# Seven-product down projection: product order, row scaling inside the last products, and weight sums on GpSimd

## The chip, the cores and the metric

The kernel runs on one core of one Trainium2 chip. The metric is the device time of one execution in microseconds. Three runs of the kernel before gave 2259.54, 2260.1 and 2260.4, median 2260.1.

## The reference, cut to what matters

One layer of a hybrid streaming encoder: a mixer (gated linear attention and retention), a residual, and a ConvFFN with a residual. The change touches only the end of the ConvFFN, for 1024 rows (SEQ) of 1024 columns (D_MODEL) and D_FF = 2816:

```
f = gelu(u_gate) * u_val
x = x + rmsnorm(f @ w_ffn_down, ln_post_ffn)
```

with `rmsnorm(y, w) = y * rsqrt(mean(y*y) + eps) * w` over the 1024 columns of a row.

## The kernel before, in words

**Seven products.** The down projection f @ w_ffn_down is done by the Strassen-Winograd scheme with seven products of half-size blocks in place of eight. f is cut into four blocks (rows 0 to 511 and 512 to 1023, D_FF halves), the weights into b11, b12, b21, b22 (D_FF halves by column halves of 512), the result into c11, c12 (rows 0 to 511) and c21, c22. A product is a sum over KH = 11 slices of 128 of D_FF. One slice of one product is a step; 77 steps (DOWN_STEPS) run in the order of DOWN_ORDER, s = 0 to 76, and `down_product(s)` gives product and slice.

**A step.** Every fp32 operand is split in a high and a low part (fp32r), and a step on TensorE is 4 groups of 128 rows (tok), each with three matmuls of 128x512 (`product3`, L433 to L435): high by high, high by low, low by high. So a step is twelve matmuls. Its parts lie in slot s % 4 of the ring w_hi and w_lo (RING = 4): ScalarE writes the high parts of weights (`w_high`, L2999) and of f (`x_high`, L3012) once the step four before is done on TensorE; VectorE writes the low parts (`w_low` L3031, `x_low` L3017; for the first steps GpSimd does the weights' in `w_low_pool` L3023).

**Sums.** Products 5, 6, 7 and 3 need sums of f blocks (`x_sum`, L3050, VectorE), products 5, 6, 7 and 4 sums of weight blocks (`w_sum`, L3069), one 128x512 subtraction a slice, written in place. VectorE does the weight sums in the order of `w_sums_at`: product 5's from step 8 on, two a step; 7's from step 13; 6's from step 21; 4's from step 56. The counters s_sum, u_sum, slab_ready, d_lo and d_hi tell the engines what is done.

**Banks.** A product accumulates in four PSUM banks, one a tok, X_BANKS or Z_BANKS. They are read out one at a time some steps behind the product: products 1 and 5 copied by ScalarE (`copies`, L3081), the others added by VectorE (`evict`, L3135 to L3146) into d_out, a view of the tile act_f. Product 4's banks are read at the very end (L3188).

**Loads.** SyncE's queue runs through `down_sp`: for each step the load of f (`x_load`, which waits until x_low of the step four before is done), and at fixed steps the rows of b22 (13 to 23, into act_f) and b21 (33 to 43, into d_b21). At step 50 it issues the residual rows, 2 MB into d_x0, waits until they are landed, and issues 2 MB more into d_x1. The eight output stores follow the last x load. f itself is stored to the scratch ffn_scratch by `f_store`, the last two blocks of it (20 and 21) from ScalarE's queue.

**Before step 8.** The up projection's last blocks run on VectorE (`taps`, `f`) between the first x_low. `up_act`, `up_dve`, `up_pool` and `up_sp` write this order out by hand; GpSimd ends there, with w_low of steps 0 to 7. Steps from 8 on are in `down_act`, `down_dve` and `down_sp`.

**The order DOWN_ORDER = (1, 5, 6, 3, 7, 2, 4).** Rows 512 to 1023 right half (c22) are done with product 7 (steps 44 to 54), rows 0 to 511 with product 2 (55 to 65), and the left half of rows 512 to 1023 (c21) with product 4 (66 to 76). For each group of 128 rows ScalarE squares the row and takes mean and root (L3087, L3094, L3098), VectorE multiplies with the weights of the norm (`weighted`, L3155), takes the reciprocal (L3150), and scales and adds the residual (`residual`, L3158). ScalarE squares the c22 halves (`half_mean`) at steps 62 to 65, and VectorE multiplies them there. The whole rows 0 to 511 (`first_rows`) are handled behind step 76, the left halves of the lower rows behind them, each as eviction on VectorE, square on ScalarE, product, reciprocal and residual on VectorE.

**The end of product 4.** TensorE runs its last four steps (73 to 76) tok by tok, so that tok 0 is done first.

Of the kernel before, what the change touches and what calls it, by code (L numbers as in the profile page):

```python
# [30 lines left out]
P = 128  # L31
# [80 lines left out]
RING = 4  # L112
# [91 lines left out]
def build(nc, x, positions, w_stream, w_dec, b_dec, ln_post_mix, ln_post_ffn, ln_cols_in, conv_in,  # L204
          ident_in, interval_in, masks_in, ret_dec_in, ret_q_in, ret_k_in, inv_freq_in, eps_in, out):
    ctx = ExitStack()
    with ctx:
# [2626 lines left out]
        def w_operand(s):  # L2834

            i, k = down_product(s)
            return {1: b11, 5: b11, 6: b11, 7: b12, 3: lambda k: d_b22[:, k, :],
                    2: lambda k: d_b21[:, k, :], 4: lambda k: d_b21[:, k, :]}[i](k)
# [18 lines left out]
        W_SUMS = [what for s in range(DOWN_STEPS) for what in w_sums_at(s)]  # L2857

        def t_sums_done(i, k):

            return AFTER_ROWS["u_sum"] + sum_count(FT - 1, 4) + W_SUMS.index((i, k)) + 1

        def evicted(i, tok, second=0):

            return {6: 2 * tok + second, 3: 8 + tok, 7: 12 + 2 * tok + second, 2: 20 + tok, 4: 24 + tok}[i] + 1
# [82 lines left out]
        def down_bank(i, tok):  # L2948
            return psum[:, (X_BANKS if i in (1, 6, 7, 4) else Z_BANKS)[tok], :]

        def down_pe(pe):
# [11 lines left out]
            def bank_free(i, tok):  # L2963
# [88 lines left out]
        def w_sum(dve, i, k):  # L3052

            if i == 5:
                dve.wait_ge(sem["slab_ready"], SL_DOWN + down_at(1, k) + 1)
                o, a, b = b11(k), b12(k), b11(k)
            elif i == 6:
                dve.wait_ge(sem["slab_ready"], SL_DOWN + down_at(5, k) + 1)
                w_landed(dve, "b22", k)
                o, a, b = b11(k), d_b22[:, k, :], b11(k)  # L3060
            elif i == 7:
                w_landed(dve, "b22", k)
                dve.wait_ge(sem["u_sum"], t_sums_done(5, k))
                o, a, b = b12(k), d_b22[:, k, :], b12(k)
            else:
                dve.wait_ge(sem["slab_ready"], SL_DOWN + down_at(2, k) + 1)
                dve.wait_ge(sem["u_sum"], t_sums_done(6, k))
                o, a, b = d_b21[:, k, :], d_b21[:, k, :], b11(k)
            nc.vector.tensor_tensor(o, a, b, ALU.subtract).then_inc(sem["u_sum"], 1)  # L3069

        def down_act(act):

            def copies(s):

                tok = (s - RING) % KH
                i = DOWN_ORDER[(s - RING) // KH - 1]
                if s < KH + RING or tok >= 4 or i not in (1, 5):
                    return
                rows = slice(HALF, D) if i == 5 else slice(0, HALF)
                step_done(act, s - RING - tok - 1)  # L3080
                nc.scalar.activation(d_out[:, (4 if i == 5 else 0) + tok, rows], down_bank(i, tok), ACT.Copy  # L3081
                                     ).then_inc(sem["u_s1"], 1)
# [8 lines left out]
            def half_mean(tok):  # L3091
                act.wait_ge(sem["d_evac"], evicted(7, tok))
                square(tok, d_out[:, 4 + tok, HALF:], 48 + tok)
# [7 lines left out]
            def first_rows(t):  # L3101
                act.wait_ge(sem["d_evac"], evicted(2, t))
                square(4 + t, d_out[:, t, :], 24 + t)
                deviation(t, eps_col[:, 0:1])

            for s in range(POOL_STEPS, DOWN_STEPS):
# [13 lines left out]
        def down_dve(dve):  # L3120
            every, first, second = slice(0, D), slice(0, HALF), slice(HALF, D)

            def evict(s):

                tok = (s - RING) % KH
                i = DOWN_ORDER[(s - RING) // KH - 1]
                if s < KH + RING or tok >= 4 or i not in (6, 3, 7, 2):
                    return
                step_done(dve, s - RING - tok - 1)
                o = down_bank(i, tok)  # L3130
                c11, c12 = d_out[:, tok, first], d_out[:, tok, second]
                c21, c22 = d_out[:, 4 + tok, first], d_out[:, 4 + tok, second]
                if i == 6:
                    dve.wait_ge(sem["u_s1"], AFTER_ROWS["u_s1"] + FT + 4 + tok + 1)
                    nc.vector.tensor_tensor(c21, o, c11, ALU.add).then_inc(sem["d_evac"], 1)  # L3135
                    dve.wait_ge(sem["d_evac"], evicted(6, tok))
                    nc.vector.tensor_tensor(c22, c22, c21, ALU.add).then_inc(sem["d_evac"], 1)
                elif i == 3:
                    dve.wait_ge(sem["d_evac"], evicted(6, tok, 1))
                    nc.vector.tensor_tensor(c12, o, c22, ALU.add).then_inc(sem["d_evac"], 1)  # L3140
                elif i == 7:
                    dve.wait_ge(sem["d_evac"], evicted(3, tok))
# [18 lines left out]
            for s in range(POOL_STEPS, DOWN_STEPS):  # L3161
# [4 lines left out]
                w_low(dve, s)  # L3166
                x_low(dve, s)
                for i, k in w_sums_at(s):
                    w_sum(dve, i, k)
                evict(s)  # L3170
                tok = s - down_at(2) - 7
                if 0 <= tok < 4:
                    dve.wait_ge(sem["d_sq"], NT + tok + 1)
                    weighted(tok, d_out[:, 4 + tok, second], d_out[:, 4 + tok, second], second)
            for t in range(4):
                dve.wait_ge(sem["d_sq"], NT + 4 + t + 1)
                weighted(4 + t, d_out[:, t, :], d_out[:, t, :], every)
            dve.wait_ge(sem["d_x_in"], 16 * MG + 32)
            for t in range(4):
                rstd(t)  # L3180
                dve.wait_ge(sem["d_scaled"], NT + 4 + t + 1)
                residual(t, d_x0, every)
# [114 lines left out]
        def up_sp(sp):  # L3297
# [18 lines left out]
            for s in range(RING, POOL_STEPS):  # L3316
# [15 lines left out]
        def up_pool(pool):  # L3332
# [111 lines left out]
        def up_act(act):  # L3444
# [58 lines left out]
            f_store(act, FT - 2)  # L3503
# [7 lines left out]
            f_store(act, FT - 1)  # L3511
# [11 lines left out]
        def up_dve(dve):  # L3523
# [96 lines left out]
            x_low(dve, RING + 3)  # L3620
            f(FT - 1)
# [141 lines left out]
```

## Time and profile before

| | us |
|---|---|
| median of three runs | 2260.1 |
| the profiled execution | 2260.02 |
| its span | 2257.8 |
| last stretch without a matmul | 20.2 |

| engine, over the whole span | busy us | share |
|---|---|---|
| TensorE, matmul (PE) | 2193.3 | 97% |
| TensorE, weight load (PEld) | 1813.0 | 80% |
| VectorE (DVE) | 1301.1 | 58% |
| ScalarE (ACT) | 713.8 | 32% |
| GpSimd (POOL) | 1433.5 | 63% |

How to read it: the span is cut by engine and by line of the kernel. The down projection takes the last 244 us, from 2014 on. Matmuls are pipelined: one is 0.39 us long in the records, and the next begins 0.23 later, so the starts are to be read, not the lengths. The same holds in part for VectorE, ScalarE and GpSimd, whose instructions overlap the next by some hundredths. `x2` is two instructions merged in one row, with the time of both. What stands in brackets is idle time of the engine before the row, and what ended it.

### The profile page before, as it was taken

How to read it: one execution, taken by the hardware profiler on the slowest of the kernel's cores; microseconds unless marked ns; L12 is line 12 of the kernel's file. 1: busy time of each engine (PE TensorE's matmuls, PEld its weight loads, DVE VectorE, ACT ScalarE, POOL GpSimd, SP SyncE). 2: the span in 40 equal slices, each digit the busy share in tenths (PEclk: the TensorE clock that was granted, in tenths of full speed). 3: DMA queues.
4: the chain of work that ended last, by engine and by line, in shares of the span. 5: the costliest groups of instructions: out<-in, count | busy, mean ns of one | idle time of the engine just before them, and what ended most of it. 6: DMA issues, size and time to landing. Idle time of an engine off the chain costs nothing. (4 is left out here: it accounts for less than half of the span.)

```text
span 2257.8 us, 27976 instructions
## 1 busy us (share of the span) xinstructions
PE 2193.3 (97%) x10354; PEld 1813.0 (80%) x10354; DVE 1301.1 (58%) x1612; ACT 713.8 (32%) x1155; POOL 1433.5 (63%) x946
## 2 busy tenths in 40 slices
PE   8999999999999999999998999999899999999996
PEld 7888888889778888877775888878778888877875
DVE  7322222222626666678887443333967777779976
ACT  4323333321222222212223111015444444444443
POOL 5787777766456555489764478860999999960000
PEclk9999999999999999999999999999999999999998
DMA  4233333323372333366556566643122222346642
GB/s 180 97 118 104 112 112 109 107 94 112 115 247 89 126 122 126 99 198 183 178 176 199 189 209 230 217 163 121 66 75 84 84 84 85 93 177 210 200 168 109
DMA packets 182613, 314.14 MB, mean 139 GB/s; under 512 B 13072, under 2 KB 93200, under 8 KB 182480
## 3 DMA queue, kind: packets, MB, share of 16 engines
q1 hardware_dynamic: 182048, 311.25, 42.4%
q8 instruction: 84, 1.38, 0.3%
q10 hardware_dynamic: 432, 1.11, 0.1%
q14 instruction: 49, 0.40, 0.1%
HBM read 222.14 MB, written 90.18 MB: 138 GB/s over the span
## 5 line engine op out<-in xcount | busy, mean ns | idle before, releaser
L433 PE MATMUL psum<-act_hi,w_hi 128*128 128x512 f32 x1272 | 505.3, 397 | 4.8 <-DVE act_lo L2291 1.4
L435 PE MATMUL psum<-act_hi,w_lo 128*128 128x512 f32 x1272 | 497.0, 391 | 0.0
L434 PE MATMUL psum<-act_lo,w_hi 128*128 128x512 f32 x1272 | 496.1, 390 | 0.0
L433 PEld LDWEIGHTS psum<-act_hi,w_hi 128*128 128x128 f32 x1272 | 239.4, 188 | 56.0 <-issue 2.9
L435 PEld LDWEIGHTS psum<-act_hi,w_lo 128*128 128x128 f32 x1272 | 239.2, 188 | 51.0
L434 PEld LDWEIGHTS psum<-act_lo,w_hi 128*128 128x128 f32 x1272 | 239.6, 188 | 46.7
L467 POOL TENSOR_TENSOR w_hi<-w_raw,zero_col 128x1024 fp32r<-128x1024 f32 x53 | 108.9, 2055 | 173.6 <-PE psum L435 154.9
L470 POOL TENSOR_TENSOR w_lo<-w_raw,w_hi 128x1024 fp32r<-128x1024 f32 x53 | 144.3, 2723 | 4.2
L1074 POOL TENSOR_TENSOR w_lo<-w_raw,w_hi 128x512 fp32r<-128x512 f32 x80 | 105.0, 1313 | 65.0 <-ACT w_hi L1032 65.0
L433 PE MATMUL psum<-w_hi,act_hi 128*128 128x512 f32 (+1 forms) x384 | 139.7, 364 | 1.7 <-POOL w_lo L470 1.4
L434 PE MATMUL psum<-w_lo,act_hi 128*128 128x512 f32 (+1 forms) x384 | 139.3, 363 | 0.0
L435 PE MATMUL psum<-w_hi,act_lo 128*128 128x512 f32 (+1 forms) x384 | 139.2, 363 | 0.0
L1584 POOL TENSOR_TENSOR k_lev<-e_t,g_x 128x896 f32<-128x896 f32 x32 | 67.3, 2103 | 104.6 <-DVE q_g L1663 64.1
L433 PE MATMUL psum<-w_hi 128*128 128x512 f32 x308 | 122.3, 397 | 8.2 <-DVE w_lo L3017 7.7
L3366 POOL TENSOR_TENSOR w_lo<-w_raw,w_hi 128x512 fp32r<-128x512 f32 x80 | 126.5, 1592 | 2.9 <-ACT w_hi L3431 2.8
L433 PE MATMUL psum<-a_sums,w_hi 128*128 128x512 f32 x320 | 124.5, 389 | 0.0
L434 PE MATMUL psum<-a_sums,w_hi 128*128 128x512 f32 x320 | 124.5, 389 | 0.0
L435 PE MATMUL psum<-a_sums,w_lo 128*128 128x512 f32 x320 | 124.5, 389 | 0.0
L434 PE MATMUL psum<-w_lo,w_hi 128*128 128x512 f32 x308 | 121.3, 394 | 0.0
L435 PE MATMUL psum<-w_hi,w_lo 128*128 128x512 f32 x308 | 121.1, 393 | 0.0
L2291 DVE TENSOR_TENSOR act_lo<-a_raw,act_hi 128x512 fp32r<-128x512 f32 x48 | 55.0, 1172 | 94.7 <-ACT act_hi L2285 94.3
L433 PE MATMUL psum<-s_hi,w_hi 128*128 128x512 f32 x264 | 103.5, 392 | 4.6 <-POOL w_lo L3366 2.1
(356 smaller groups left out, 5094.1 us busy)
## 6 DMA issues: line engine op xcount, KB each, us to landing
w_raw<-in_w_stream SPq DMA_DIRECT2D x181, 512.0 KB, 4.4
proj_scratch<-stage SPq DMA_DIRECT2D x40, 512.0 KB, 5.2
r_x<-proj_scratch SPq DMA_DIRECT2D x64, 256.0 KB, 3.7
w_raw<-ffn_scratch SPq DMA_DIRECT2D x55, 256.0 KB, 2.7
value_scratch<-stage SPq DMA_DIRECT2D x24, 512.0 KB, 3.6
proj_scratch<-side_out SPq DMA_DIRECT2D x48, 256.0 KB, 2.4
w_raw<-ffn_scratch SPq DMA_DIRECT2D x22, 512.0 KB, 4.2
ffn_scratch<-u_lin_v SPq DMA_DIRECT2D x20, 512.0 KB, 5.8
```

The lines of the kernel that those rows point to most:

```text
L433: nc.tensor.matmul(o, s_hi, m_hi, start=start, stop=False)
L434: nc.tensor.matmul(o, s_hi, m_lo, start=False, stop=False)
L435: return nc.tensor.matmul(o, s_lo, m_hi, start=False, stop=stop)
L467: nc.gpsimd.tensor_tensor(w_hi[:, j, :], w_raw[:, j, :], zero_col[:, :].to_broadcast((P, D)), ALU.add).then_inc(sem["hi_split"], 1)
L470: nc.gpsimd.tensor_tensor(w_lo[:, j, :], w_raw[:, j, :], w_hi[:, j, :].bitcast(F32), ALU.subtract).then_inc(sem["slab_ready"], 1)
L1074: nc.gpsimd.tensor_tensor(w_lo8[:, n % 8, :], row_block(p, i), w_hi8[:, n % 8, :].bitcast(F32), ALU.subtract).then_inc(sem["u_lo"], 1)
L1584: nc.gpsimd.tensor_tensor(by_chunk(k_lev, b), level_decays(b), every_level(key), ALU.mult).then_inc(sem["g_klev"], 1)
L2291: nc.vector.tensor_tensor(lo, a_raw[:, i % RING, :], hi.bitcast(F32), ALU.subtract).then_inc(sem["a_lo"], 1)
L3366: nc.gpsimd.tensor_tensor(w_lo8[:, n % 8, :], block_raw(p, i), w_hi8[:, n % 8, :].bitcast(F32), ALU.subtract).then_inc(sem["u_lo"], 1)
```

## The change

1. DOWN_ORDER becomes (1, 5, 6, 3, 2, 7, 4): product 2 now at steps 44 to 54, product 7 at 55 to 65. Products 1, 6, 2, 4 use the X banks, 5, 3, 7 the Z banks, and the banks of each lie in neighbouring pairs.
2. GpSimd splits the low parts of the weights up to step 10 (POOL_STEPS = 11), and then makes all weight sums, in `w_sum`, two slices an instruction (128x1024; the eleventh slice alone, 128x512): 24 instructions in place of 44 on VectorE. The sum for product 4 goes into b11's place and no longer into b21's.
3. ScalarE's copies and VectorE's evictions read two banks at once, 1024 wide.
4. The rows of the residual are loaded 128 at a time, four loads at steps 48 to 51 and four at 56 to 59, none waiting for another.
5. Squares and roots of rows 0 to 511 (`first_rows`) are at steps 61 to 64, their multiplications at 62 to 65, reciprocal and residual at 66 to 69. The squares of the c22 halves and their multiplications are behind step 76.
6. The stores of f blocks 20 and 21 go from ScalarE's queue to SyncE's, behind the x loads of steps 9 and 11. x_low of step 8 is put ahead of f of block 21 on VectorE.

```diff
-        DOWN_ORDER = (1, 5, 6, 3, 7, 2, 4)
+        DOWN_ORDER = (1, 5, 6, 3, 2, 7, 4)
-        X_BANKS, Z_BANKS = (6, 7, 1, 2), (3, 0, 4, 5)
-        POOL_STEPS = 2 * RING
+        X_BANKS, Z_BANKS = (6, 7, 0, 1), (2, 3, 4, 5)
+        EARLY_STEPS = 2 * RING
+        POOL_STEPS = 11
+        IN_X = (1, 6, 2, 4)
...
+        def b1_pair(k):
+
+            if k < 2:
+                return d_b1_first[:, 0:2, :]
+            return d_b1_mid[:, k - 2:k, :] if k < 10 else d_b1_last[:, :].unsqueeze(1)
...
-        def w_sums_at(s):
-
-            at = [(5, k) for k in range(KH) if k // 2 == s - POOL_STEPS]
-            at += [(i, s - start) for i, start in ((7, KH + 2), (6, 2 * KH - 1), (4, 5 * KH + 1))
-                   if start <= s < start + KH]
-            return at
...
+        W_SUMS_AT = {9: ((5, 0), (5, 2)), 10: ((5, 4), (5, 6)), 11: ((5, 8),), 12: ((5, 10),),
+                     16: ((7, 0),), 18: ((7, 2),), 20: ((7, 4),), 45: ((7, 6),), 47: ((7, 8),), 49: ((7, 10),),
+                     21: ((6, 0),), 23: ((6, 2),), 25: ((6, 4),), 27: ((6, 6),), 29: ((6, 8),), 31: ((6, 10),),
+                     46: ((4, 0),), 48: ((4, 2),), 50: ((4, 4),), 52: ((4, 6),), 53: ((4, 8),), 54: ((4, 10),)}
+        W_SUMS = [what for s in sorted(W_SUMS_AT) for what in W_SUMS_AT[s]]
...
-        def residual_rows(sp, hf):
-            sp.dma_start((d_x1 if hf else d_x0)[:, :, :],
-                         x1_d[hf * HALF:hf * HALF + HALF, :].rearrange("(t p) d -> p t d", p=P)
+        def residual_rows(sp, t):
+            sp.dma_start((d_x1 if t >= 4 else d_x0)[:, t % 4, :], x1_d[t * P:(t + 1) * P, :]
...
+                if s in (9, 11):
+                    f_store(sp, FT - 2 if s == 9 else FT - 1)
...
-                if s == 4 * KH + RING + 2:
+                if 4 * KH + 4 <= s < 4 * KH + 8:
+                    sp.wait_ge(sem["s_sum"], s_sums(3, KH - 1))
+                    residual_rows(sp, s - 4 * KH)
+                if 5 * KH + 1 <= s < 5 * KH + 5:
                     sp.wait_ge(sem["slab_ready"], SL_DOWN + 4 * KH)
                     sp.wait_ge(sem["u_sum"], t_sums_done(7, KH - 1))
-                    sp.wait_ge(sem["s_sum"], s_sums(3, KH - 1))
-                    residual_rows(sp, 0)
-                    sp.wait_ge(sem["d_x_in"], 16 * MG + 16)
-                    residual_rows(sp, 1)
+                    residual_rows(sp, s - 5 * KH - 1)
...
+        def w_sum(pool, i, k):
+
+            n = min(2, KH - k)
+            slab = b1_pair(k)
+            first, second = slab[:, :, 0:HALF], slab[:, :, HALF:]
+            b22, b21 = d_b22[:, k:k + n, :], d_b21[:, k:k + n, :]
             if i == 5:
+                pool.wait_ge(sem["slab_ready"], SL_DOWN + down_at(1, k + n - 1) + 1)
+                o, a, b = first, second, first
             elif i == 6:
+                pool.wait_ge(sem["slab_ready"], SL_DOWN + down_at(5, k + n - 1) + 1)
+                for m in range(k, k + n):
+                    w_landed(pool, "b22", m)
+                o, a, b = first, b22, first
             elif i == 7:
+                for m in range(k, k + n):
+                    w_landed(pool, "b22", m)
+                pool.wait_ge(sem["u_sum"], t_sums_done(5, k))
+                o, a, b = second, b22, second
             else:
+                for m in range(k, k + n):
+                    w_landed(pool, "b21", m)
+                pool.wait_ge(sem["slab_ready"], SL_DOWN + down_at(6, k + n - 1) + 1)
+                pool.wait_ge(sem["u_sum"], t_sums_done(6, k))
+                o, a, b = first, b21, first
-            nc.vector.tensor_tensor(o, a, b, ALU.subtract).then_inc(sem["u_sum"], 1)
+            nc.gpsimd.tensor_tensor(o, a, b, ALU.subtract).then_inc(sem["u_sum"], 1)
...
-                if down_at(2) + 7 <= s < down_at(2) + 11:
-                    half_mean(s - down_at(2) - 7)
-            for t in range(4):
-                first_rows(t)
+                if 61 <= s < 65:
+                    first_rows(s - 61)
+            for tok in range(4):
+                half_mean(tok)
...
             for s in range(POOL_STEPS):
                 w_low_pool(pool, s)
+            for i, k in W_SUMS:
+                w_sum(pool, i, k)
...
             gelu(FT - 2)
             w_high(act, RING + 1)
             x_high(act, RING + 1)
-            f_store(act, FT - 2)
...
             x_low(dve, RING + 3)
+            x_low(dve, EARLY_STEPS)
             f(FT - 1)
```

## Rows read from the trace of the kernel before

**Rows 1.** Busy time by stretch: from:to, length, each engine's busy us, PEclk, DMA share, GB/s

```profile
2041.23:2080.56 39.33, 39.19 (x168) 31.28 (x169) 39.13 (x66) 17.64 (x33) 0.00 (x0) 1.00 0.77 255
2161.26:2166.31 5.05, 5.05 (x12) 3.96 (x13) 5.05 (x9) 1.78 (x3) 0.00 (x0) 0.52 0.50 156
2166.31:2237.64 71.33, 71.16 (x313) 58.30 (x311) 53.88 (x84) 36.80 (x71) 0.00 (x0) 1.00 0.24 79
2237.64:2257.80 20.16, 0.00 (x0) 0.00 (x0) 13.86 (x22) 4.07 (x12) 0.00 (x0) 0.59 0.51 206
```

**Rows 2.** Timeline of TensorE: start us, us, engine, line, operation, out<-in, count [idle before]

```profile
2080.56 0.39 PE L433 MATMUL psum<-w_hi 128*128 128x512 f32 x1
...
2156.49 0.39 PE L435 MATMUL psum<-w_hi,w_lo 128*128 128x512 f32 x1
2161.26 0.76 PE L433 MATMUL psum<-w_hi 128*128 128x512 f32 x1 [4.38 <-DVE w_lo L3017]
```

**Rows 3.** Timelines of VectorE and SyncE's queue around the residual loads

```profile
2147.37 0.69 DVE L3017 TENSOR_TENSOR w_lo<-w_raw,w_hi 128x512 fp32r<-128x512 f32 x1
...
2159.22 0.69 DVE L3050 TENSOR_TENSOR w_raw<-w_raw 128x512 f32<-128x512 f32 x1 [10.56 <-DMA w_raw<-ffn_scratch]
...
2140.36 0.37 SPq L2914 DMA_DIRECT2D act_f<-x_scratch  x1
2150.08 0.37 SPq L2914 DMA_DIRECT2D d_x<-x_scratch  x1
2150.50 10.96 SPq L2895 DMA_DIRECT2D w_raw<-ffn_scratch  x4
```

**Rows 4.** Timelines of VectorE and ScalarE: the tail, and one half square

```profile
2240.76 0.68 DVE L3188 TENSOR_TENSOR act_f<-psum,act_f 128x512 f32<-128x512 f32 x1
...
2251.70 0.68 DVE L3188 TENSOR_TENSOR act_f<-psum,act_f 128x512 f32<-128x512 f32 x1
...
2189.41 0.61 ACT L3087 ACTIVATE d_junk<-act_f 128x512 f32<-128x512 f32 x1
...
2190.15 0.29 ACT L3094 ACTIVATE stat<-stat,eps_col 128x1 f32<-128x1 f32 x1
...
2227.49 1.04 ACT L3087 ACTIVATE d_junk<-act_f 128x1024 f32<-128x1024 f32 x1
```

**Rows 5.** Timeline of VectorE in product 5, GpSimd idle

```profile
2052.44 1.29 DVE L3069 TENSOR_TENSOR d_b_mid<-d_b_mid 128x512 f32<-128x512 f32 x2
2053.64 0.69 DVE L3050 TENSOR_TENSOR d_s_lo<-w_raw 128x512 f32<-128x512 f32 x1
```

**Rows 6.** Timelines of GpSimd and VectorE where both run, and VectorE alone (1519.79)

```profile
1939.21 1.30 POOL L3366 TENSOR_TENSOR w_lo<-u_t,w_hi 128x512 fp32r<-128x512 f32 x1
1940.46 3.54 POOL L3366 TENSOR_TENSOR w_lo<-w_raw,w_hi 128x512 fp32r<-128x512 f32 x2
...
1940.66 2.20 DVE L3565 SCALAR_TENSOR_TENSOR u_lin_g<-u_cg,conv_col,u_lin_g 128x1023 f32<-128x1023 f32 x1 [1.36 <-ACT u_lin_g L3457]
1942.89 2.20 DVE L3568 SCALAR_TENSOR_TENSOR u_lin_g<-u_cg,conv_col,u_lin_g 128x1022 f32<-128x1022 f32 x1
...
1497.94 2.40 POOL L2528 TENSOR_TENSOR w_lo<-w_raw,w_hi 128x1024 fp32r<-128x1024 f32 x1
...
1498.34 4.15 DVE L2553 TENSOR_TENSOR act_lo<-m_raw,act_hi 128x2048 fp32r<-128x2048 f32 x1 [10.86 <-ACT act_hi L2547]
...
1519.79 2.29 DVE L2553 TENSOR_TENSOR m_lob<-m_raw,m_hib 128x2048 fp32r<-128x2048 f32 x1 [3.35 <-ACT m_hib L2547]
```

**Rows 7.** Timelines of VectorE and ScalarE at the last block of the up projection

```profile
2037.22 1.21 DVE L3575 TENSOR_TENSOR u_lin_v<-u_lin_v,u_lin_g 128x1024 f32<-128x1024 f32 x1
...
2027.26 0.34 ACTq L3295 DMA_DIRECT2D ffn_scratch<-u_lin_v  x1
2027.72 1.24 ACT L3457 ACTIVATE u_lin_g<-u_cg,conv_col 128x1024 f32<-128x1024 f32 x1 [3.98 <-DVE u_lin_v L3575]
```

**Rows 8.** DMA issues: out<-in, engine, count, KB each, median us to landing

```profile
d_b<-in_w_stream SPq DMA_DIRECT2D x11, 256.0 KB, 3.9
```

More of the change, by code:

```diff
@@ L2848, in s_sums, with copied @@
             return 16 + (5, 6, 3, 7).index(i) * KH + k + 1
-        def w_sums_at(s):
-            at = [(5, k) for k in range(KH) if k // 2 == s - POOL_STEPS]
-            at += [(i, s - start) for i, start in ((7, KH + 2), (6, 2 * KH - 1), (4, 5 * KH + 1))
-                   if start <= s < start + KH]
-            return at
-        W_SUMS = [what for s in range(DOWN_STEPS) for what in w_sums_at(s)]
+        W_SUMS_AT = {9: ((5, 0), (5, 2)), 10: ((5, 4), (5, 6)), 11: ((5, 8),), 12: ((5, 10),),
[3 rows of a table added]
+        W_SUMS = [what for s in sorted(W_SUMS_AT) for what in W_SUMS_AT[s]]
         def t_sums_done(i, k):
-            return AFTER_ROWS["u_sum"] + sum_count(FT - 1, 4) + W_SUMS.index((i, k)) + 1
+            return AFTER_ROWS["u_sum"] + sum_count(FT - 1, 4) + W_SUMS.index((i, k // 2 * 2)) + 1
         def evicted(i, tok, second=0):
-            return {6: 2 * tok + second, 3: 8 + tok, 7: 12 + 2 * tok + second, 2: 20 + tok, 4: 24 + tok}[i] + 1
+            q = tok // 2
+            return {6: 2 * q + second, 3: 4 + q, 2: 6 + q, 7: 8 + 2 * q + second, 4: 12 + tok}[i] + 1
+        def copied(i, tok):
+            return AFTER_ROWS["u_s1"] + FT + {1: 0, 5: 2}[i] + tok // 2 + 1
         def x_landed(eng, s):
@@ L3076, in copies @@
                 i = DOWN_ORDER[(s - RING) // KH - 1]
-                if s < KH + RING or tok >= 4 or i not in (1, 5):
+                if s < KH + RING or q >= 2 or odd or i not in (1, 5):
                     return
                 rows = slice(HALF, D) if i == 5 else slice(0, HALF)
-                step_done(act, s - RING - tok - 1)
-                nc.scalar.activation(d_out[:, (4 if i == 5 else 0) + tok, rows], down_bank(i, tok), ACT.Copy
-                                     ).then_inc(sem["u_s1"], 1)
+                t = (4 if i == 5 else 0) + 2 * q
@@ L3084, in square @@
+                step_done(act, s - RING - 2 * q - 1)
+                nc.scalar.activation(d_out[:, t:t + 2, rows], down_banks(i, q), ACT.Copy).then_inc(sem["u_s1"], 1)
             def square(n, rows, into):
@@ L3102, in first_rows @@
                 act.wait_ge(sem["d_evac"], evicted(2, t))
-                square(4 + t, d_out[:, t, :], 24 + t)
+                square(t, d_out[:, t, :], 24 + t)
                 deviation(t, eps_col[:, 0:1])
-            for s in range(POOL_STEPS, DOWN_STEPS):
+            for s in range(EARLY_STEPS, DOWN_STEPS):
                 w_high(act, s)
@@ L3159, in residual @@
                                                x[:, t % 4, cols], ALU.mult, ALU.add).then_inc(sem["d_res"], 1)
-            for s in range(POOL_STEPS, DOWN_STEPS):
+            for s in range(EARLY_STEPS + 1, DOWN_STEPS):
                 if s == KH - 1:
@@ L3165, in down_dve @@
                     x_sum(dve, s + 1)
-                w_low(dve, s)
+                if s >= POOL_STEPS:
+                    w_low(dve, s)
                 x_low(dve, s)
-                for i, k in w_sums_at(s):
-                    w_sum(dve, i, k)
                 evict(s)
[L3171 to L3182, printed above, removed]
+                if 62 <= s < 66:
+                    t = s - 62
+                    dve.wait_ge(sem["d_sq"], NT + t + 1)
+                    weighted(t, d_out[:, t, :], d_out[:, t, :], every)
+                if 66 <= s < 70:
+                    t = s - 66
+                    if t == 0:
+                        dve.wait_ge(sem["d_x_in"], 16 * MG + 16 * NT)
+                    rstd(t)
+                    dve.wait_ge(sem["d_scaled"], NT + t + 1)
+                    residual(t, d_x0, every)
+            for tok in range(4):
+                dve.wait_ge(sem["d_sq"], NT + 4 + tok + 1)
+                weighted(4 + tok, d_out[:, 4 + tok, second], d_out[:, 4 + tok, second], second)
             for tok in range(4):
@@ L3315, in up_sp @@
                 w_load(sp, "b1", k)
-            for s in range(RING, POOL_STEPS):
+            for s in range(RING, EARLY_STEPS):
                 x_load(sp, s)
```

53 lines of the change are left out of this document (22 added, 31 removed).

## The prediction

> **What bounds the kernel now.** Read first the busy time by stretch [rows 1]. From 2041 to 2080 us TensorE and VectorE are both full and GpSimd does nothing; from 2166 to 2238 VectorE is at 76% and TensorE runs without a hole; the last 20.2 us have no matmul. So three things set the end: TensorE's own 77 steps, the places where it waits, and the tail. The matmul timeline prices them [rows 2]. Between 2080.56 (first matmul of step 22) and 2156.49 lie 335 matmuls, 0.2267 us each, so a step of twelve is 2.72. Then comes a hole: 2161.26 instead of 2156.72, 4.5 us, and the step behind it takes 5.05 us instead of 2.72, at a granted clock of 0.52, the 1.2 GHz level [rows 1], another 2.3. The hole costs 6.9. The VectorE and SyncE timelines name its cause [rows 3]: VectorE waited 10.56 us for an x load that SyncE issued only when the first 2 MB residual load had landed (issued 2140.36, the next at 2150.08), and that then queued behind the second. They also show VectorE's lead: the low part of step 49 was there at 2148.06, and its twelve matmuls, of which the one at 2156.49 is the last, began at 2154.0. So x_low comes 5.9 us before TensorE needs it, when VectorE keeps up; the ring of four slots allows no more. Last the tail [rows 4]: VectorE starts the first of the last four evictions at 2240.76, though its product was done some 11 us earlier, because rows 0 to 3 are finished first; the last one starts at 2251.70 and the end follows 6.1 us later.
>
> **The tail: 9.1 us gained.** Rows 0 to 3 need products 1, 6, 5, 3 and 2. With product 2 ahead of 7, they are complete at step 61, and their squares, weights and residuals go into steps 61 to 69. What is left behind the loop is four half squares on ScalarE and four half-width multiplications. ScalarE starts there at 2227.49 as now; a half square to the end of its mean takes 1.03 (2189.41 to 2190.44), in a row about 0.95, and the multiplication follows the accumulator (0.8 after the start), so the fourth ends near 2227.5 + 3×0.95 + 0.8 + 0.6 = 2231.7. The last evictions then start at 2231.7 and not 2240.76, and their pace (10.94 for three) stays, for it is a chain of both engines; TensorE's last tokens are 2.72 apart, faster than that. Gain 9.1. The moved work fits: in steps 62 to 65 VectorE has 3×0.6 + 1.2 = 3.0 per step of 2.72, which takes 1.2 of the lead of 5.9. The one table load moves to step 61, where ScalarE is half free (36.8 of 71.3 us busy [rows 1]). With that cover gone, each us would be one on TensorE.
>
> **The residual loads: 6.9 gained.** Eight loads of 512 KB replace two of 2 MB, none waits for the other, and SyncE's own waits (for the sums of 3 and 7) are long met by then. Four of them lie in product 7, whose x loads are 512 KB too: 1 MB a step. In [rows 3] 2.5 MB landed in 9 us, so 1 MB would take 3.6 us, 0.9 over the step, four times: at most 3.6 of lateness against a lead of 5.9. I take zero; the bound is 1.
>
> **Pair-wide evictions.** Two 512-wide instructions in a row have a pitch of 0.60 (x2 from 2052.44 to 2053.64 [rows 5]), so 1024 at once costs the same 1.2. By the Trainium skill (VectorE: DVE Perf Modes, The TRN2 errata) a fixed cost is paid per instruction, and its formula would save about 0.16 for each of the ten merged pairs, 1.6 us of VectorE in all. The row shows none of that for instructions queued one behind another; I take zero.
>
> **The sums on GpSimd: the cost.** VectorE sheds 44 subtractions of 0.60 = 26.4 us and three w_low. GpSimd gets 24 instructions, 20 of them 1024 wide. The trace shows what these do to VectorE [rows 6]. Alone, a GpSimd instruction of 1024 takes 2.40 and a 512 one 1.30. But while one runs, a VectorE instruction with both inputs in SBUF does not: one begun at 1498.34, 0.40 behind a GpSimd start, took 4.15 instead of the 2.29 of its twin at 1519.79. With both engines supplied they alternate: VectorE 1940.66 and 1942.89, 1023 wide, pitch 2.23, where alone GpSimd's 512 has a pitch of 1.25 (1939.21 to 1940.46) and two of VectorE's 512 one of 1.20 [rows 5]; so 0.23 of a pair overlaps. A 1024 sum therefore delays VectorE by about 2.36 (its 2.40 less the same step from duration to pitch) - 0.23 = 2.13, a 512 one by 1.03, where VectorE did the same two sums in 1.20. And w_low, x_low and x_sum all have two SBUF inputs.
>
> By the Trainium skill (SBUF — State Buffer, SBUF: two separate sides) the shared pair is held for the whole instruction; without the overlap of 0.23 the 24 sums and w_low would cost some 5 us more, 2270. The rows decide for the smaller price.
>
> *First knot, step 8 to 22.* Block 21's last multiplication starts at 2037.22 now [rows 7]. It comes 0.47 earlier (ScalarE no longer issues the store at 2027.26, and the activation behind it began at 2027.72), but x_low of step 8 (0.6) goes ahead of it, and w_low of steps 8 and 9, now on GpSimd, delay VectorE by 1.03 each: 2039.4. From there to the end of x_low of step 12 VectorE has 1.2 + 9×0.6 = 6.6, and GpSimd cuts in with w_low 10, the six sums of product 5 and the first of product 7, all ready: 1.03 + 5×2.13 + 1.03 + 2.13 = 14.8. That gives 2060.8. Steps 13 to 22 need 10×1.81 = 18.1 of VectorE, and the sums in line behind (two of product 7, six of 6, one more of 7; 8×2.13 + 1.03) 18.1, of which about 1 falls while VectorE waits for a load. So step 22 starts at 2096.3, against 2080.56: 15.7 late. GpSimd cannot be paced by TensorE here: its waits are for loads of the weights and for VectorE's own w_low, which are met early. The holes fall at steps 9 to 11 and 17.
>
> *Second knot, step 32 to 40.* After (7,6) GpSimd waits for b21 rows, loaded from step 33 on, and VectorE regains its full lead by step 28, since 1.81 is under 2.72. The b21 rows land 3.9 us behind their issue [rows 8]. From x_low 31 to x_low 40 VectorE has 9×1.81 + 4.8 (four wide instructions of product 6) = 21.1, and the eight remaining sums add 6×2.13 + 2×1.03 = 14.8: 35.9 where TensorE takes 24.5. The lead covers 5.9, and 5.5 is left as a hole at steps 38 to 40. Bounds: 0, if two or three sums slip behind step 40 or beside evictions that read PSUM (no row here prices that), and 8, if the clock falls behind each hole by 2.3. I take 5.5. From step 44 on VectorE has 1.2 a step and no sum: nothing further.
>
> **Sum.** The profiled execution took 2260.02 with a span of 2257.8, 2.2 around it, and is 0.1 from the median of 2260.1. -9.1 - 6.9 + 15.7 + 5.5 = +5.2, so 2265.3. A measurement of this kernel can tell about 0.2%, 4.5 us, from no change.
>
> **Rivals.**
> *The second knot is covered (0.26).* For it: the sums of 4 aren't needed before step 66, and one that arrives late delays nobody; against it: GpSimd takes them as soon as the rows land. Then -16.0 + 15.7 gives 2259.8, no change; with half of it, 2262.
> *GpSimd's sums fit into VectorE's free time (0.17), the other side.* Place: steps 9 to 22. VectorE sheds 26.4 us, and if a sum waited for idle time rather than alternated, VectorE would need 1.81 a step against 2.72 and TensorE would never wait. Price: the two gains, 16.0, and about 1.5 of present waits: 2242.5. It wins if a 1024 sum delays VectorE by less than 0.8: 14 steps with 0.91 free each, over 15.4 sums. For it: GpSimd is empty there [rows 1]; against it: every contended row of [rows 6]. With 1.5 per 1024 sum instead of 2.13 both knots shrink by 12 together: 2253.
> *The clock stays low (0.15).* Holes of 1, 2.6, 3 and 5 us follow each other within 40 us. If the 1.2 GHz level lasts for five steps behind the one at step 17 and two in the second knot, each 2.3 more, of which about 5 is in the sum's slack, TensorE becomes the later engine: +11, 2276.
> *The change doesn't move the tail (0.02)*, if rows 0 to 3 were late again: 2274.
>
> **Chances and range.** Forecast 0.40 (own range 2260 to 2270). Faster by over 0.2% (under 2255.6): the free-time rival and a little of the covered one, 0.20. Within 0.2%: 0.31. Slower (over 2264.6): 0.49. The range reaches from 2250 to 2276; most of the free-time rival and the end of the clock's stay out, 0.2.
>
> **What would show it.** GpSimd busy from 2040 to about 2095, w_sum rows near 2.4 to 3 us; VectorE's w_low and x_low beside them 2.8 and not 0.69, and still 0.69 in steps 24 to 31. Step 22 some 16 us late, holes at steps 9 to 11, 17 and 38 to 40, none at 50. From the last matmul to the end 11 us instead of 20.2. Wrong would be the first knot if x_low 12 ends before 2055; the second if no hole lies between 32 and 44; the residual part if a hole stands at 56 to 60.

## The result, and the profile after

The kernel after takes 2271.3 us (median of five, 2268.77 to 2274.53), the kernel before 2260.1 (median of five, 2257.95 to 2260.57): ratio 1.0052, 95% interval 1.0038 to 1.0067. It is slower by 11.2 us where 5.2 was predicted. The profiled execution took 2271.04 with a span of 2268.9, 11.1 more than the span before, so its trace holds the whole difference.

Read first the busy time by stretch (from:to, length, each engine's busy us, granted clock of TensorE, DMA share, GB/s), as in [rows 1]:

```profile
2041.00:2080.00 39.00, 31.53 (x121) 24.76 (x120) 38.21 (x26) 11.90 (x19) 29.79 (x12) 0.88 0.66 208
...
2041.00:2060.00 19.00, 12.61 (x46) 9.64 (x45) 18.86 (x8) 2.94 (x5) 19.00 (x8) 0.86 0.60 183
2061.80:2099.20 37.40, 31.19 (x124) 24.40 (x122) 36.74 (x31) 13.59 (x22) 23.90 (x9) 0.93 0.51 169
2099.00:2119.00 20.00, 19.70 (x87) 16.35 (x88) 17.33 (x29) 10.95 (x18) 0.00 (x0) 1.00 0.45 146
2119.00:2155.00 36.00, 31.49 (x131) 25.02 (x129) 35.27 (x30) 12.09 (x21) 20.36 (x8) 0.95 0.41 131
2145.94:2149.06 3.12, 3.12 (x7) 2.46 (x8) 3.09 (x5) 1.15 (x2) 0.00 (x0) 0.50 0.57 181
2166.00:2237.64 71.64, 71.64 (x318) 59.33 (x317) 57.05 (x83) 36.70 (x66) 0.00 (x0) 1.00 0.54 188
```

From 2041 to 2060 VectorE is busy for 18.86 us with eight instructions, 2.4 each; alone they take 0.7 to 1.2. GpSimd is busy for all 19.00, and TensorE for only 12.61. Where GpSimd has nothing (2099 to 2119), VectorE's 29 instructions take 0.6 each again and TensorE has its full 2.4 GHz. From 2119 to 2155 the picture of the start returns. From 2166 on TensorE is never idle.

The timelines of VectorE and GpSimd in the first knot show how (start us, us, engine, line, operation, out<-in, shapes):

```profile
2042.34 2.66 DVE L3032 TENSOR_TENSOR w_lo<-w_raw,w_hi 128x512 fp32r<-128x512 f32 x1
2044.92 2.89 DVE L3065 TENSOR_TENSOR d_s_lo<-w_raw 128x512 f32<-128x512 f32 x1
2047.73 2.85 DVE L3032 TENSOR_TENSOR w_lo<-w_raw,w_hi 128x512 fp32r<-128x512 f32 x1
2050.51 2.88 DVE L3065 TENSOR_TENSOR d_s_lo<-w_raw 128x512 f32<-128x512 f32 x1
...
2066.06 0.69 DVE L3065 TENSOR_TENSOR d_s_lo<-w_raw 128x512 f32<-128x512 f32 x1 [0.66 <-DMA w_raw<-ffn_scratch]
...
2098.52 0.68 DVE L3032 TENSOR_TENSOR w_lo<-d_s_lo,w_hi 128x512 fp32r<-128x512 f32 x1
...
2044.41 11.19 POOL L3092 TENSOR_TENSOR d_b_mid<-d_b_mid 128x1024 f32<-128x1024 f32 x4
```

The two engines take turns: VectorE's starts are 2.58, 2.81 and 2.78 us apart, GpSimd's four sums 2.80 each (11.19 / 4). The instruction at 2098.52 is x_low of step 22.

TensorE's own timeline answers to [rows 2]:

```profile
2084.46 0.77 PE L433 MATMUL psum<-w_hi 128*128 128x512 f32 x1 [3.19 <-DVE w_lo L3032]
...
2099.30 0.47 PE L433 MATMUL psum<-w_hi 128*128 128x512 f32 x1 [2.04 <-DVE w_lo L3046]
...
2145.94 0.77 PE L433 MATMUL psum<-w_hi 128*128 128x512 f32 x1 [2.50 <-DVE w_lo L3032]
...
2155.23 0.47 PE L433 MATMUL psum<-w_hi 128*128 128x512 f32 x1 [2.13 <-DVE w_lo L3032]
```

Each of these four holes was ended by a low part from VectorE. Step 22 starts at 2099.30 and not at 2080.56: 18.7 late. A further 8.5 us go in the second knot, 5.2 in holes ahead of steps 38 and 40 (steps counted back from the last matmul at 2.726 us each) and 3.3 in matmuls at the 1.2 GHz level behind them. Such a matmul takes 0.77 instead of 0.39.

The tail, as in [rows 4]:

```profile
2248.02 0.62 ACT L3110 ACTIVATE d_junk<-act_f 128x512 f32<-128x512 f32 x1
2248.54 0.19 ACT L3110 ACTIVATION_READ_ACCUMULATOR d_junk<-act_f 128x1 f32 x1
2248.76 0.30 ACT L3117 ACTIVATE stat<-stat,eps_col 128x1 f32<-128x1 f32 x1
2248.96 0.62 ACT L3110 ACTIVATE d_junk<-act_f 128x512 f32<-128x512 f32 x1
...
2251.59 0.69 DVE L3178 TENSOR_TENSOR act_f<-act_f,d_ln 128x512 f32<-128x512 f32 x1 [0.25 <-ACT d_junk L3110]
2252.20 0.68 DVE L3212 TENSOR_TENSOR act_f<-psum,act_f 128x512 f32<-128x512 f32 x1
...
2262.80 0.68 DVE L3212 TENSOR_TENSOR act_f<-psum,act_f 128x512 f32<-128x512 f32 x1
```

The last evictions begin at 2252.20, before the last matmul has ended (2258.2), and the end comes 10.7 us behind it, against 20.2 before. The four terms are +18.7 + 8.5 - 6.9 - 9.5 = +10.8, where the spans differ by 11.1.

### The profile page after: what moved, and what is told of

It is laid out like the page before. It is cut to its first block and busy times, and to the rows that moved or that the text cites. A ratio compares the mean times of both kernels' runs of the same rounds, so it can differ in the third digit from the quotient of the medians.

```text
span 2268.9 us, 27933 instructions
## 1 busy us (share of the span) xinstructions
PE 2199.3 (97%) x10354; PEld 1817.0 (80%) x10354; DVE 1318.1 (58%) x1553; ACT 714.5 (31%) x1151; POOL 1503.5 (66%) x973
```

## The experiments

The theory at this point: what the change costs is only that GpSimd's sums hold VectorE up in two full stretches, 18.7 and 8.5 us, and what it gains (9.5 in the tail, 6.9 at the residual loads) is independent of them. The rivals: something else in the change costs too; the sums would cost the same anywhere; it is not VectorE's and GpSimd's shared reading that matters.

### The weight sums back on VectorE

The kernel after, everything kept but the engine of the weight sums:

```diff
+        W_SUMS_AT = {s: () for s in range(DOWN_STEPS)}
+        for k in range(KH):
+            for i, at in ((5, 9 + k // 2), (7, 13 + k), (6, 2 * KH - 1 + k), (4, 45 + k)):
+                W_SUMS_AT[at] += ((i, k),)
...
-            nc.gpsimd.tensor_tensor(o, a, b, ALU.subtract).then_inc(sem["u_sum"], 1)
+            nc.vector.tensor_tensor(o, a, b, ALU.subtract).then_inc(sem["u_sum"], 1)
...
                 x_low(dve, s)
+                for i, k in W_SUMS_AT[s]:
+                    w_sum(dve, i, k)
...
-            for i, k in W_SUMS:
-                w_sum(pool, i, k)
```

> The kernel after with the weight sums back on VectorE, as 44 subtractions of 512 (those of product 5 two a step from step 9, of 7 from step 13, of 6 from 21, of 4 from 45); all else as after. Theory (the sums on GpSimd are the whole cost: 18.7 us up to step 22, 8.5 in the second knot): VectorE has about 1.81 + 0.60 to 1.20 a step, both knots shrink to under 3 us together, and tail and residual loads keep their 9.5 and 6.9: 2242 to 2248. Rival (the order of products, the tail's work in steps 61 to 69 or the pair-wide evictions cost as well): 2250 to 2262. No w_low or x_low between 2042 and 2100 us longer than 0.75 under the theory, but for the few beside GpSimd's last w_low's.

Measured: 2244.44 us (2242.39 to 2247.51), ratio to before 0.9928 (0.9912 to 0.9945). Busy time by stretch:

```profile
2041.00:2080.00 39.00, 38.10 (x163) 30.02 (x162) 37.88 (x64) 16.93 (x28) 0.00 (x0) 1.00 0.80 267
2119.00:2155.00 36.00, 36.00 (x160) 29.85 (x159) 28.23 (x43) 15.01 (x26) 0.00 (x0) 1.00 0.51 181
```

From 2041 to 2080 VectorE does 64 instructions (the sums among them) where beside GpSimd it did 26, with the sums on the other engine, and TensorE is busy for 38.10 us instead of 31.53. The theory holds: 26.9 us less than the kernel after by the medians, 28 by the ratios, and the two knots were 27.2. Order of the products, tail and wide evictions cost nothing that can be seen.

### The late sums spread over later steps

The kernel after, with the last nine sums held back:

```diff
             for i, k in W_SUMS:
+                if i == 4 or (i == 7 and k >= 6):
+                    step_done(pool, {(7, 6): 40, (4, 0): 41, (7, 8): 42, (4, 2): 43, (7, 10): 44, (4, 4): 45,
+                                     (4, 6): 47, (4, 8): 48, (4, 10): 49}[(i, k)])
                 w_sum(pool, i, k)
```

> The kernel after, where GpSimd's sums from (7, 6) on wait for TensorE to finish steps 40 to 49, one or two steps apart, instead of starting as soon as their rows are loaded. Theory (the second knot is only a matter of when these eight sums run: in steps 33 to 40 VectorE is full, from 44 on it has 1.2 us of work a step): the three holes near 2137 to 2160 us go, -8.5: 2261 to 2264. Rival (the sums cost VectorE the same wherever they run, and the lead isn't there later either): holes of 2 to 8 us appear at steps 50 to 60, 2268 to 2274. Second rival: the sums come too late for product 7 (step 55) or 4 (step 66): slower than after.

Measured: 2261.98 us (2259.53 to 2265.34), ratio 1.0006 (0.9996 to 1.0015): 9.3 less than the kernel after. Busy time of the stretch that held it, and the next, then three rows of the timelines of VectorE and GpSimd:

```profile
2119.00:2155.00 36.00, 36.00 (x160) 29.84 (x159) 29.18 (x39) 15.39 (x27) 5.32 (x3) 1.00 0.43 146
2155.00:2180.00 25.00, 23.29 (x102) 18.66 (x101) 25.00 (x20) 9.99 (x18) 16.38 (x7) 1.00 0.49 174
...
2172.52 2.88 DVE L3032 TENSOR_TENSOR w_lo<-w_raw,w_hi 128x512 fp32r<-128x512 f32 x1
2175.32 1.21 DVE L3163 TENSOR_TENSOR act_f<-psum,act_f 128x1024 f32<-128x1024 f32 x1
...
2174.80 1.74 POOL L3092 TENSOR_TENSOR d_b_last<-d_b,d_b_last 128x512 f32<-128x512 f32 x1
```

TensorE does not stop from 2119 to 2155, and behind that it is idle for 1.7 us (25.00 - 23.29) in two short holes, although VectorE is busy for all of those 25 us. With the matmuls behind these holes that is 2.2 us where the second knot had 8.5; another 2.2 went because (7, 6) has left the first knot, and with it the hole ahead of step 22, which starts at 2097.11 and not at 2099.30. Together they are the 8.5 us by which the two profiled spans differ. So the theory's total was right and a part of it came from elsewhere than written. Nearly the same sums (eight, and nine with (7, 6)) cost 8.5 us or 2.2 by their place alone; the rival of an equal cost anywhere falls. The last three rows price what the prediction found no row for: the eviction at 2175.32, which reads PSUM, keeps its 1.21 us beside a running GpSimd sum, where w_low or x_low would be held. The trace of before had such rows too: the additions at 1938.02 and 1938.62, which read PSUM, take 0.68 us beside GpSimd's w_low from 1937.96 to 1940.52. The last experiment but one adds eight more.

### GpSimd writes and doesn't read

```diff
-            nc.gpsimd.tensor_tensor(o, a, b, ALU.subtract).then_inc(sem["u_sum"], 1)
+            nc.gpsimd.memset(o, 0.0).then_inc(sem["u_sum"], 1)
```

> The kernel after with each of GpSimd's 24 subtractions replaced by a fill of the same output with zeros, at the same place and under the same waits. Left out: the sums of the weights, so products 5, 6, 7 and 4 multiply zeros. It writes the same SBUF columns and reads none. Theory (what holds VectorE up is that two instructions with two SBUF inputs each can't run at once): w_low and x_low beside a fill stay at 0.69, both knots go, 2240 to 2248. Rival (whatever GpSimd does in SBUF holds VectorE up, by its length): the rows beside it are as long as the fill plus 0.4, and the time follows the fill's length: with fills of 2.4 us 2268 to 2272, with fills of half that about 2256. Multiplying zeros may also change what TensorE is granted; its clock before 2040 us is the measure.

Measured: 2243.11 us (2240.87 to 2246.23), ratio 0.9922. Timelines of GpSimd and VectorE:

```profile
2040.03 3.64 POOL L3092 MEMSET d_b_mid<- 128x1024 f32 x4
...
2040.41 0.69 DVE L3032 TENSOR_TENSOR w_lo<-w_raw,w_hi 128x512 fp32r<-128x512 f32 x1
2041.02 0.69 DVE L3065 TENSOR_TENSOR d_s_lo<-w_raw 128x512 f32<-128x512 f32 x1
2041.62 0.69 DVE L3032 TENSOR_TENSOR w_lo<-w_raw,w_hi 128x512 fp32r<-128x512 f32 x1
```

Four fills of 0.91 us run one behind another, and VectorE's three instructions beside them start 0.61 and 0.60 apart, as if alone. So GpSimd writing the same columns does not hold VectorE up. The rival, by the length of the fills, would have wanted VectorE rows of 1.3. The zeros did not change what TensorE was granted either: 0.91 of its clock from 2020 to 2040 and 1.00 from 2041 to 2080, the same as with the copies of the next experiment.

### GpSimd reads one input

```diff
-            nc.gpsimd.tensor_tensor(o, a, b, ALU.subtract).then_inc(sem["u_sum"], 1)
+            nc.gpsimd.tensor_copy(o, b).then_inc(sem["u_sum"], 1)
```

> The kernel after with each of GpSimd's 24 subtractions replaced by a copy of its second input into the same output, under the same waits. Left out: the differences of the weights (products 5, 6, 7 and 4 multiply the copied blocks). GpSimd now reads one input instead of two and writes as before. Theory A (only two instructions with two SBUF inputs each exclude one another): w_low and x_low stay at 0.69 beside the copies: 2242 to 2247. Theory B (any GpSimd read of SBUF excludes a VectorE instruction with two inputs): the rows beside a copy are as long as the copy plus 0.4, as beside a sum; with copies of 1.0 to 2.4 us the time is 2252 to 2271.

Measured: 2243.65 us (2241.51 to 2245.67), ratio 0.992 (0.9904 to 0.9935). Timelines of GpSimd and VectorE:

```profile
2043.20 5.39 POOL L3092 COPY d_b_mid<-d_b_mid 128x1024 f32<-128x1024 f32 x4
...
2043.72 1.52 DVE L3065 TENSOR_TENSOR d_s_lo<-w_raw 128x512 f32<-128x512 f32 x1
2045.17 1.52 DVE L3032 TENSOR_TENSOR w_lo<-w_raw,w_hi 128x512 fp32r<-128x512 f32 x1
```

Here the time alone would mislead: it lies in theory A's band, but the rows are theory B's. VectorE's start is 1.45 behind the one before instead of 0.60, so a copy with a single input does hold VectorE up. It is only short: 1.35 us for 1024 columns (5.39 / 4, with VectorE idle beside a part of them), a delay of 1.45 - 0.60 = 0.85 against a sum's 2.2. Theory A is refuted as to what excludes what. The time then tells how much delay per instruction these stretches bear: 24 meetings of at most 0.85 leave TensorE one more hole of 1.2 us (at 2049 to 2051) and no loss that the time shows.

### Sums of 512 columns

Two of GpSimd's instructions in place of each wide one:

```diff
-            n = min(2, KH - k)
-            slab = b1_pair(k)
-            first, second = slab[:, :, 0:HALF], slab[:, :, HALF:]
-            b22, b21 = d_b22[:, k:k + n, :], d_b21[:, k:k + n, :]
+            n = 1
+            first, second = b11(k), b12(k)
+            b22, b21 = d_b22[:, k, :], d_b21[:, k, :]
```

> The kernel after with each of GpSimd's 1024-wide sums cut into two of 512 (44 instructions in place of 24, the same elements). Theory (the price goes by GpSimd's busy time less an overlap of 0.23 per meeting of the two engines): 20 more meetings, each with a pitch 0.0 to 0.1 longer for GpSimd and 0.23 more overlap: 2x1.03 to 2x1.15 for a pair instead of 2.11, so 2268 to 2272, w_low and x_low beside it 1.7 instead of 2.8. Rival (VectorE takes its turn between two GpSimd instructions, whatever their length, so that shorter ones leave it half of the turns): GpSimd needs twice as many turns, each w_low or x_low waits 1.1 instead of 2.2, the sums are spread over more steps into VectorE's free time behind step 22: 2262 to 2267.

Measured: 2268.6 us (2266.35 to 2272.26), ratio 1.0032 (1.0022 to 1.0043; the kernel after has 1.0038 to 1.0067). Timelines of GpSimd and VectorE:

```profile
2045.41 13.57 POOL L3091 TENSOR_TENSOR d_b_mid<-d_b_mid 128x512 f32<-128x512 f32 x8
...
2049.32 1.78 DVE L3046 TENSOR_TENSOR w_lo<-act_f,w_hi 128x512 fp32r<-128x512 f32 x1
2051.03 1.75 DVE L3032 TENSOR_TENSOR w_lo<-d_s_lo,w_hi 128x512 fp32r<-128x512 f32 x1
2052.70 1.77 DVE L3065 TENSOR_TENSOR d_s_lo<-w_raw 128x512 f32<-128x512 f32 x1
```

Both engines go at 1.70 a turn (13.57 / 8; 2051.03 to 2052.70 is 1.67), so one sum delays VectorE by 1.70 - 0.60 = 1.10, two by 2.20. A wide one delays it by 2.80 - 0.60 = 2.20. The price goes by columns, and the rows and the time are as the theory had them. The rival has in its favour that the median is 2.7 us lower than the kernel after; the two intervals overlap, and whether that is anything stays open.

### The residual loads alone

The kernel before with only this part of the change:

```diff
-                if s == 4 * KH + RING + 2:
+                if 4 * KH + RING + 2 <= s < 4 * KH + RING + 10:
                     sp.wait_ge(sem["slab_ready"], SL_DOWN + 4 * KH)
                     sp.wait_ge(sem["u_sum"], t_sums_done(7, KH - 1))
                     sp.wait_ge(sem["s_sum"], s_sums(3, KH - 1))
-                    residual_rows(sp, 0)
-                    sp.wait_ge(sem["d_x_in"], 16 * MG + 16)
-                    residual_rows(sp, 1)
+                    residual_rows(sp, s - 4 * KH - RING - 2)
```

> The kernel before with its two 2 MB residual loads cut into eight of 512 KB, one a step from step 50 to 57, none waiting for another; nothing else. Theory (the hole at step 54 and the step at 1.2 GHz behind it come from the wait of the second residual load for the first): the 10.56 us wait of VectorE and the hole near 2161 us go, -6.9: 2252 to 2255, and the tail of 20.2 us stays. Rival (the 4 MB themselves take the time, and the hole is spread over steps 51 to 59): 2257 to 2261.

Measured: 2253.22 us (2252.49 to 2254.49), ratio 0.9966 (0.9953 to 0.9979): -7.6, with an interval from -4.7 to -10.6, within the theory's band. Busy time of the stretch that answers to the second line of [rows 1]:

```profile
2155.00:2166.00 11.00, 11.00 (x51) 9.09 (x50) 7.00 (x12) 4.61 (x8) 0.00 (x0) 1.00 0.83 296
```

No hole, full clock (the hole of before stands ahead of step 50, counted from [rows 2], and not of step 54 as expected above), and the same 4 MB pass beside the x loads at a DMA share of 0.83. The wait cost the time and not the bytes. (The two profiled spans differ by 5.4 us only, for this execution is already 1.5 behind at step 6, 2034.93 against 2033.43, ahead of anything that was changed.) What the kernel with the sums on VectorE has beyond this one, 0.9928 against 0.9966 or 8.6 us, is what is left of the change: mainly the tail, predicted at 9.1.

### The sums alone in the kernel before

Its 44 sums of 512 on GpSimd, in the old order, behind the first eight w_low; the function's body stays, only the engine changes:

```diff
             for s in range(POOL_STEPS):
                 w_low_pool(pool, s)
+            for i, k in W_SUMS:
+                w_sum(pool, i, k)
...
-                for i, k in w_sums_at(s):
-                    w_sum(dve, i, k)
```

> The kernel before with only one part of the change: its 44 weight sums of 512 on GpSimd, in their old order, under their old waits. Theory (a 512 sum delays VectorE by 1.10, wherever the alternation runs without a gap): from 2041 us 33 sums stand in line, 1.70 each with the VectorE instruction between, to about 2097; VectorE does 33 instructions in that time, which takes it to step 19 of TensorE's; step 20 then starts some 23 us later than in before, and behind it VectorE is free again. The sums of product 4 come behind step 55, one a step, 1.2 + 1.1 us, with up to 4 us lost beside the evictions: 2283 to 2288, the hole at step 54 as in before. Rival (the loss here is smaller than the 27 us of the changed kernel, because the hole at step 54 takes part of it): 2276 to 2280.

Measured: 2278.91 us (2278.04 to 2283.43), ratio 1.0081 (1.0066 to 1.0097). That is +18.0 and under the 2283 to 2288 expected. Timeline of GpSimd in the first knot, and timelines of GpSimd and VectorE beside the sums of product 4:

```profile
2058.64 1.47 POOL L3069 TENSOR_TENSOR act_f<-act_f 128x512 f32<-128x512 f32 x1 [2.05 <-DMA act_f<-in_w_stream]
2061.87 1.75 POOL L3069 TENSOR_TENSOR d_b_mid<-act_f,d_b_mid 128x512 f32<-128x512 f32 x1 [1.76 <-DMA act_f<-in_w_stream]
...
2088.41 13.55 POOL L3069 TENSOR_TENSOR d_b_mid<-act_f,d_b_mid 128x512 f32<-128x512 f32 x8
...
2190.38 1.67 POOL L3069 TENSOR_TENSOR d_b<-d_b,act_f 128x512 f32<-128x512 f32 x1 [86.71 <-DVE w_lo L3031]
...
2201.25 1.68 POOL L3069 TENSOR_TENSOR d_b<-d_b,d_b_mid 128x512 f32<-128x512 f32 x1 [1.05 <-DVE w_lo L3031]
...
2212.42 1.68 POOL L3069 TENSOR_TENSOR d_b<-d_b,d_b_mid 128x512 f32<-128x512 f32 x1 [1.32 <-DVE w_lo L3031]
...
2201.70 0.68 DVE L3143 TENSOR_TENSOR act_f<-psum,act_f 128x512 f32<-128x512 f32 x1
2202.30 0.68 DVE L3144 TENSOR_TENSOR act_f<-psum,act_f 128x512 f32<-128x512 f32 x1
...
2212.86 1.78 DVE L3155 TENSOR_TENSOR act_f<-act_f,d_ln 128x512 f32<-128x512 f32 x1
```

The price was right: from 2042.03 to 2104.13 VectorE does 49 instructions without a pause, 30 of them long, (62.1 - 49x0.60) / 30 = 1.09 each. What was expected of the line of waiting sums was not. Eight sums of product 7 each waited 0.9 to 2.4 us for their rows of the weights, 12.5 us together, between 2056 and 2080, and in these VectorE did its short instructions undisturbed. TensorE starts step 24, behind its last hole there, at 2104.36, where by [rows 2] before starts it at 2086.00 (24 matmuls of 0.227 behind 2080.56): 18.4 us later, not 23. Behind that GpSimd rests for 86.7 us, the hole at the residual loads stands as before (6.35 against 4.54), and the sums of product 4, one a step behind step 55, cause none. The last rows show one reason: the eight evictions beside these sums, with one input in PSUM, keep their 0.68 us, while the multiplication at 2212.86, with both inputs in SBUF, takes 1.78. The rival's number fits; its reason does not, for the hole at the residual loads took nothing off, it grew by 1.8. So the first knot costs about the same here as in the changed kernel (18.4 and 18.7), though by another path, and the 26.9 us there are this one and the second knot, which comes only with the early sums of product 4.

### Two low parts more on VectorE

The kernel with the sums on VectorE (first experiment), with `POOL_STEPS` 9:

```diff
-        POOL_STEPS = 11
+        POOL_STEPS = 9
```

> The kernel with the weight sums on VectorE (2244.4 us), where the low parts of the weights of steps 9 and 10 go back from GpSimd to VectorE as well. Theory (a 512-wide GpSimd instruction delays VectorE by about 1.1, its own costs it 0.60): block 21's last multiplication starts 0.5 to 1.5 us sooner than 2037.61, the holes of 0.96 and 0.78 us near 2036 and 2057 shrink by 0.5 to 1 in all: 2243 to 2244. Rival (VectorE has no time in steps 9 to 14, which hold 3.0 us a step already): the hole at 2057 grows by 1.2: 2245 to 2246.

Measured: 2242.86 us (2238.41 to 2244.51), ratio 0.9916 (0.9902 to 0.9929). Timelines of VectorE and GpSimd:

```profile
2037.33 1.21 DVE L3592 TENSOR_TENSOR u_lin_v<-u_lin_v,u_lin_g 128x1024 f32<-128x1024 f32 x1
2038.75 0.69 DVE L3046 TENSOR_TENSOR w_lo<-d_b_mid,w_hi 128x512 fp32r<-128x512 f32 x1 [0.21 <-issue]
...
2031.71 4.55 POOL L3038 TENSOR_TENSOR w_lo<-d_b_mid,w_hi 128x512 fp32r<-128x512 f32 x2 [0.56 <-ACT w_hi L3014]
```

GpSimd has ended at 2036.26, and block 21's last multiplication takes 1.21 instead of 2.31 us: it ends 1.4 sooner, while the two w_low cost VectorE 1.2. The holes after 2037 are gone, but the one that ends near 2037 has grown from 1.0 to 2.3 us, where the theory had it shrink. The 1.2 GHz level costs both kernels about the same: here 3 us of matmuls behind that hole run at it (0.54 from 2037.8 to 2041.4), in the first experiment as many behind the hole before (0.55 from 2031.7 to 2035.5). The two profiled spans are equal, 2240.6. The median is 1.6 lower than with `POOL_STEPS` 11, as the theory has it, but the intervals overlap: not told apart. It has the lowest median of the study, 0.84% under the kernel before.

## Why the prediction was right, and where its terms were off

The sign, the range of 2250 to 2276 and the mechanism held. The size did not hold as well: the predicted 2265.3 was 6.0 too low, the change costs 11.2 us and not 5.2, and the forecast's own range of 2260 to 2270 was missed by 1.3. Of the 6.0, each knot holds 3.0. By its own steps:

**The tail: predicted -9.1, measured -9.5.** The half squares come 0.94 to 0.95 apart (2248.02, 2248.96), the multiplications follow them, and the fourth ends where the last evictions begin. The work moved into steps 61 to 69 made no hole: TensorE is busy for 71.64 of 71.64 us there. Shown by the trace, and by what the first experiment has beyond the residual loads.

**The residual loads: predicted -6.9, measured -7.6** alone on the kernel before; no hole at steps 50 to 60 in the kernel after. Shown.

**Pair-wide evictions: predicted 0.** Two of them in a row start 1.13 apart (2232.69 and 2233.82), where two 512-wide instructions took 1.20 [rows 5]. By the Trainium skill (VectorE: DVE Perf Modes, The TRN2 errata) the fixed cost of the instruction saved would give about 0.16 each, an estimate from its formula; the trace shows some 0.07, and on a stretch where VectorE isn't what TensorE waits for.

**First knot: predicted +15.7, measured +18.7.** The step that failed is "18.1, of which about 1 falls while VectorE waits for a load". VectorE did wait (the row at 2066.06 is the only one), but no sum ran in that wait: GpSimd stood idle for 6.8 us up to 2066.87, ahead of its second sum of product 7 (in the runs with fills and copies the same idle time is ended by the load of that sum's rows). So 0.74 us came on top of the sums where 1 was to come off: 1.7 of the 3.0. The rest is the price of a sum, 2.20 and not 2.13, 1.10 and not 1.03, about 1.1 over the 17 instructions of GpSimd up to step 22. Then block 21's multiplication starts at 2039.91 and not 2039.4, 0.5; and TensorE follows x_low 0.1 behind, where the predicted 2096.3 lies 0.3 over its own terms, -0.2. Worked out again from measured rows, the stretch from 2061.8 to 2099.2 closes: 30x0.60 + 8x2.19 + 1.10 + 0.74 = 37.4. The holes lie ahead of steps 10, 11, 17, 18 and 22, near the 9 to 11 and 17 forecast.

**The price's form.** The overlap of 0.23 a pair, taken from 1023-wide instructions of VectorE [rows 6], was 0.16 here. By the Trainium skill (SBUF — State Buffer, SBUF: two separate sides) the shared pair is held for the whole of an instruction: a turn would then be at least 2.36 + 0.60 = 2.96, an estimate. The rows show 2.80, between this and the predicted 2.73 and nearer to the latter; the measurement decides.

**Second knot: predicted +5.5, measured +8.5.** The holes were sized right, 5.2 at steps 38 to 40. What was left out of the value taken, though named for its bound of 8, is TensorE at 1.2 GHz behind both holes: 3.3. The 8.5 measured lie above that bound too. In the first knot the same clock (0.52 from 2057.9 to 2063.9) cost nothing of its own, because VectorE was the later engine there; in the second VectorE had caught up and nothing hid it. That "VectorE has 1.2 a step and no sum" from step 44 on is what the second experiment used, and it bore nine sums there for 2.2 us. The prediction's "no row here prices that", of evictions beside GpSimd, is wrong: the rows at 1938.02 and 1938.62 do, at no delay.

**The rivals.** "The sums fit into VectorE's free time" put its point at a delay of 0.8 a sum and its time at 2242.5. With copies, at 0.85, the kernel takes 2243.65: the point was right, and the sums are at 2.2. "The second knot is covered" (2259.8) came true only when the sums were placed for it (2261.98). "The clock stays low" did not: it came back 3 to 6 us behind each hole.

## What to carry to other kernels

Work moved from a full VectorE to an idle GpSimd is not moved if GpSimd reads SBUF and VectorE has both inputs there: a 1024-wide subtraction that VectorE does in 1.2 us cost it 2.2 as a bystander. Compare what the helper's instruction takes from the other engine, column for column, with what the engine sheds, before looking at how idle the helper is. If it must be there, its place decides: the late sums cost 8.5 us in steps without slack and 2.2 ten steps later, so pace the helper by the engine it must not disturb. And split a change into its parts: this one held 16 us of gain under 27 us of loss.

## What the runs showed of the hardware

- GpSimd reading SBUF, with one input or two, and VectorE instructions with both inputs in SBUF exclude one another and take turns: 2.80 us a turn with 1024-wide sums, 1.70 with 512-wide ones, 1.45 with 1024-wide copies. A GpSimd fill (0.91 for 1024 columns) holds nothing up, and VectorE evictions with one input in PSUM ran through beside a sum: 1.21 once in the second experiment, 0.68 eight times in the one with the sums alone in the kernel before. An instruction of VectorE with a single SBUF input and no PSUM one was not tried.
- In the kernel after, of TensorE's nine holes of over 1 us from 2030 on, the granted clock was at the 1.2 GHz level behind five: those of 2.3 (twice), 2.7, 3.3 and 4.3 us, for 3.1 to 6.0 us. Behind four of 2.2 (twice), 2.4 and 1.2 it was not. Other runs show that the length alone does not tell: the low level stood behind holes of 2.1 (first experiment, 2031.03) and 2.2 (second, 2033.20), and not behind one of 2.2 (last, 2031.84). From 2.1 to 2.4 us the rows hold both.
